# A first block's gates and output matrix, and a first mixer's output matrix, in three passes of rounded parts, with a ring of five slots for the opening's last sixteen

## The chip, the cores and the metric

The kernel runs on one core of one Trainium2 chip, in one launch. The metric is the device time of that core in microseconds (us), the median of three runs.

## The reference, cut to what matters

Two transformer-like blocks over 256 tokens of width 1024, all in float32. The first block runs once; its gates and its output matrix are the last two lines of its mixer:

```python
h = rms_norm(x, norm1_g[l]) * (1.0 + sc1) + sh1
z = h @ w_in[l]
u_val, u_gate, q, k, v, f_logit, gate_c, gate_a = split(z)
conv_out = conv_module(u_val, u_gate, ...)           # 31 taps, layer norm, silu, matrix
attn_out = forgetting_attention(q, k, v, f_logit + b_forget) @ w_attn_out[l]
mixed = sigmoid(gate_c) * conv_out + sigmoid(gate_a) * attn_out
x = x + g1 * (mixed @ w_out[l])
h2 = rms_norm(x, norm2_g) * (1.0 + sc2) + sh2
x = x + g2 * moe_ffn(h2, ...)                        # 32 experts, 4 for each token
```

The second block has two layers. Each is a hybrid mixer (windowed attention and a two-way retention, whose outputs are gated, added and multiplied with `w_out`), then a dense feed-forward part in the first layer and 8 experts in the second.

## The kernel before, in words

The activations stand feature-major: a tile holds 1024 features as 8 pieces of 128 partitions by 256 tokens. Every engine has its own instruction list, written out by hand, and semaphores order them.

**The stream of weight slots.** `plan()` lists the dense matrices in the order of use, cut into slots of 1 MiB (128 x 2048 float32). SP loads them in that order into a ring in the tile `W` (L458): 15 slots for the 50 slots of the first block (the opening), 5 slots from the second block on. A slot is loaded when its predecessor in the ring is free (`free_at`), and since SP works in order, a slot that has to wait holds up all behind it. The opening's stream is 8 slots of `ada0`, then `uqkv_a` (6) and `uqkv_b` (4) with `ada1` and `ada2` (8 each) between them, then `gates` (8), `attn_out` (2), `conv_out` (2) and `w_out` (4): 34 slots and then 16.

**Jobs.** A job multiplies one slot (or half of one) with the activations into one PSUM bank; two banks alternate, and the job after next waits until the bank is read. `feature_job` (L676 to L702) has two forms. A plain one takes float32 operands as they are (L702: 16 products, which the profile shows as 32 matmuls). A split one (L691) takes rounded parts: ACT copies the slot into `WHI_D` in a rounded format (L405), POOL subtracts that from the slot into `WLO_D` (L409, four instructions of 128 x 512), the activations stand likewise in `XHI` and `XLO`, and TensorE makes three passes, high by high, low by high and high by low (48 matmuls). There are four buffers of `WHI_D` and `WLO_D`; the counter `lin_done` counts jobs, `dense_hi` and `dense_lo` count slots split. Before, all split matrices belong to the second block (qa, kva, ret, gg, ffn1, ffn3, ffn2); for them the same memory is laid out as 5 raw slots, 4 high buffers (places 5 to 8 of the ring of 15), 4 low buffers (9 to 12), `XHI` (13) and `XLO` (14).

**The opening.** TensorE runs uqkv, forget, ada(2), and then a hand-written loop over ten steps: a gates job, every second step the attention scores of two heads (L919 to L928), then the values (L948) and the turned probabilities (L937). The scores wait for `negf_ready`, which VectorE (DVE) gives at the end of `log_sigmoid` (L1818 to L1831) and a scan (L2020, L2021). DVE also makes the `ada` products (L1947) and the 31 taps of the convolution, 4 instructions each (L2006): 8 taps just ahead of `log_sigmoid`, and 2 in each step of the loop. ACT reads the banks out (L1549, L1561), and makes the exponentials. Then come attn_out and conv_out, whose products DVE gates (L2069) and adds (L2072), and the four jobs of w_out, with a norm behind them.

**The experts of the first block.** `experts1` (SP, L467): an expert has 12 groups of 1 MiB (8 of `w_exp_in`, 4 of `w_exp_out`), which lie in ring places 3 to 14: groups 0 to 9 in places 5 to 14, groups 10 and 11 in places 3 and 4. The first expert's groups are loaded when the last slot of the stream in that place is free; then SP loads 3 slots of the second block (places 0 to 2), waits for the routing tables, and from there loads group s of the next expert when TensorE has used group s of the expert before (all its chunks). TensorE takes each expert in chunks of 64 tokens: products with the groups at L1102.

**The first mixer** (`mixer2(0)`): after gates and heads, wo_attn (2 slots, 4 jobs) and wo_ret (2 slots, 4 jobs), whose products DVE gates (L2417) and adds (L2439), then w_out0 (4 plain jobs), a first sum behind job 1 (L782), and a norm whose squares go with the later jobs (L1858, L2350, L1861, L2353, L2338, L791). Then ffn1.

```python
def split_dense(eng, q):
    n, _ = split_slots[q]
    if q >= SPLIT_N:
        eng.wait_ge(sem("lin_done"), split_slots[q - SPLIT_N][1])
```

Of the kernel before, what the change touches and what calls it, by code (L numbers as in the profile page):

```python
# [20 lines left out]
F32 = mybir.dt.float32  # L21
# [26 lines left out]
RING = 15  # L48
# [12 lines left out]
class Linear:  # L61


    def __init__(self, name, slots, jobs_per_slot, evac, k_major=0):
# [3 lines left out]
        self.split = name.rstrip("01") in ("qa", "kva", "ret", "gg") or name in ("ffn1", "ffn3", "ffn2")  # L68


def plan():
# [51 lines left out]
    return lins, job_evac, stream, free_at, n_block1, split_slots  # L123
# [17 lines left out]
def build_two_blocks(nc, A, out):  # L141
    lins, job_evac, stream, free_at, N_A, split_slots = plan()
    N_SLOTS = len(stream)
    ctx = ExitStack()
    with ctx:
# [64 lines left out]
        def slot(n):  # L210
            r = n % RING if n < N_A else (n - N_A) % RING2
# [180 lines left out]

        def split_dense(eng, q):
# [54 lines left out]
        def _(sp):  # L448
# [14 lines left out]
            def experts1():  # L463
# [5 lines left out]
                for s in range(12):  # L469
                    wait_free(last_in_ring(ring1(s)))  # L470
# [14 lines left out]
            def experts2():  # L485
# [23 lines left out]
                sp.wait_ge(sem("mix_ready"), 12)  # L509
# [36 lines left out]
        def _(pool):  # L546
# [48 lines left out]
            def mixer2(l):  # L595
                q0 = 52 * l
                for q in range(q0, q0 + 11):
                    if q in (0, 1):
                        pool.wait_ge(sem("m1_split_room"), q + 1)
                    if q == 2:  # L600
                        pool.wait_ge(sem("normed"), 10)
                    split_dense(pool, q)
                for h in range(HEADS):
# [8 lines left out]
                        .then_inc(sem("decay_masked"), 1)  # L612
                    split_dense(pool, q0 + 11 + h)
# [9 lines left out]
                i.then_inc(sem("pool_tables"), 1)  # L623

# [4 lines left out]

            slot_iota(m1)  # L630
            mixer2(0)
            for q in range(19, 52):
# [8 lines left out]
        def _(pe):  # L641
# [38 lines left out]
            def feature_job(lin, s, x, nk=KT, part=0, width=256, ready=None):  # L680

                job = lin.job0 + s * lin.per + part
                if lin.split:
                    q = split_ready(lin, s)
                    bank_free(job)
                    for j in range(width // P):
                        c = part * width + j * P
                        for i, (w, xp) in enumerate(PASSES):
                            w = w[:, q % SPLIT_N, :].rearrange("p (k n) -> p k n", k=KT)
                            for k in range(KT):  # L690
                                mm = pe.matmul(ps(job % 2, T, c0=j * T), w[:, k, c:c + P], xp[:, k, :],  # L691
# [263 lines left out]
            for i in range(10):  # L955
                if i < 8:
                    feature_job(lin, i, H)
# [20 lines left out]
            pe.wait_ge(sem("mix_ready"), 4)  # L978

# [12 lines left out]
            for s in range(4):  # L992
                feature_job(lins["w_out"], s, z(GC, GC + 8))
# [276 lines left out]
            def mixer2(l):  # L1270
# [111 lines left out]
                for s in range(4):  # L1382
                    feature_job(lin, s, z(G2A, G2A + 8), ready=("mix_ready", 4 * l + 5) if s == 0 else None)
# [1140 lines left out]
```

## Time and profile before

| | us |
|---|---|
| median of 3 runs (2340.43 to 2341.96) | 2341.57 |
| the profiled execution's own time | 2340.47 |
| its span in the profile | 2338.7 |
| TensorE busy | 2244.8 (96%) |
| VectorE, ScalarE, GpSimd busy | 714.5, 620.8, 394.1 |
| stage: opening, to the end of w_out | 0 to 262.5 |
| stage: routing and experts of the first block | 262.5 to about 1253 |
| stage: first mixer, to the end of its w_out | about 1280 to 1477 |

The sum of the prediction is made against the profiled execution (2340.47), which is 1.1 us under the median. The clock granted to TensorE is full in nearly the whole span (mean 0.987). The busy shares are averages over stages with different limits, and a busy TensorE can be one with a slow clock, so each stage is read by itself.

### The profile page before, as it was taken

The numbers are of one execution on the slowest core, as the hardware profiler recorded it, in microseconds if no ns is written. First come the engines' busy times: TensorE is split into PE (matmuls) and PEld (weight loads), VectorE is DVE, ScalarE is ACT, GpSimd is POOL, SyncE is SP. The second block draws the span as 40 slices with busy tenths as digits, with TensorE's granted clock in tenths as the row PEclk, the third lists the DMA queues.
The fourth block names the chain that finished last, engine by engine and source line by source line (L and its number), as shares of the span: only waits on it lengthen the run. The fifth ranks groups of instructions, "written<-read, shape, count | busy, mean of one in ns | idle before, by whom it ended". The sixth has DMA issues, their size and how long they took to land.

```text
span 2338.7 us, 36205 instructions
## 1 busy us (share of the span) xinstructions
PE 2244.8 (96%) x13812; PEld 1373.0 (59%) x13813; DVE 714.5 (31%) x1376; ACT 620.8 (27%) x903; POOL 394.1 (17%) x371
## 2 busy tenths in 40 slices
PE   7999999999999999999998999999999999999898
PEld 5887744444444444444446988899998863333333
DVE  4864322222222222222225244312315341111013
ACT  2143111111111111112124671443458011111111
POOL 2000000000000000000003761688586000000000
PEclk9999999999999999999999999999999999999999
DMA  9973399999999999989994533555454475999652
GB/s 359 381 259 110 101 411 418 418 418 418 418 418 418 417 418 418 418 363 380 418 418 167 179 109 108 180 183 180 127 180 117 155 287 216 402 405 396 276 230 84
DMA packets 223487, 688.71 MB, mean 294 GB/s; under 512 B 28330, under 2 KB 117362, under 8 KB 187570
## 3 DMA queue, kind: packets, MB, share of 16 engines
q1 hardware_dynamic: 221776, 685.82, 76.4%
q10 hardware_dynamic: 1490, 1.61, 0.2%
q8 instruction: 56, 0.92, 0.2%
q0 software_dynamic: 144, 0.20, 0.0%
q14 instruction: 21, 0.17, 0.0%
HBM read 686.53 MB, written 1.05 MB: 294 GB/s over the span
## 4 chain that ended last, share of the span: by engine, by line
PE 72%; DMA 11%; SPq 11%; DVE 3%; issue 2%; ACT 1%; POOL 0%; ACTq 0%; DVEq 0%; POOLq 0%
PE PS L1102 17%; PE PS L702 12%; DMA RAW<-in_w_exp_in 10%; PE PS L691 6%; SPq L467 6%; PE PS L1206 6%; PE PS L676 6%; PE PS L1066 4%; PE PS L1217 3%; SPq L489 3%; PE PS L1407 3%; PE PS L1085 2%; PE PS L748 1%; PE PS L1113 1%; SPq L497 1%
## 5 line engine op out<-in xcount | busy, mean ns | idle before, releaser
L1102 PE MATMUL PS<-RAW,Z 128*64 128x512 f32 x3168 | 713.3, 597 | 24.1 <-DMA RAW<-in_w_exp_in 23.2
L409 POOL TENSOR_TENSOR WLO_D<-W,WHI_D 128x512 fp32r<-128x512 f32 x284 | 360.2, 1304 | 1159.6 <-ACT SPARE L1632 965.9
L1102 PEld LDWEIGHTS PS<-RAW,Z 128*64 128x64 f32 x3168 | 213.7, 136 | 454.7 <-issue 376.8
L1206 PE MATMUL PS<-W,Z 128*64 128x512 f32 (+1 forms) x1056 | 212.5, 558 | 10.9 <-DMA W<-in_moe_w 10.2
L702 PE MATMUL PS<-Z,W 128*128 128x256 f32 x768 | 170.1, 382 | 1.5 <-DVE Z L2072 1.5
L405 ACT ACTIVATE WHI_D<-W 128x2048 fp32r<-128x2048 f32 x71 | 135.3, 1908 | 114.0 <-DMA W<-in_ffn_w 42.3
L1206 PEld LDWEIGHTS PS<-W,Z 128*64 128x64 f32 x1056 | 74.5, 137 | 148.9 <-issue 129.6
L702 PEld LDWEIGHTS PS<-Z,W 128*128 128x128 f32 x768 | 146.4, 191 | 23.0 <-DVE Z L2072 1.9
L1066 PE MATMUL PS<-Z 128*128 128x64 f32 x1088 | 125.3, 273 | 0.0
L1066 PEld LDWEIGHTS PS<-Z 128*128 128x128 f32 x1088 | 124.2, 192 | 0.2 <-issue 0.2
L2194 DVE TENSOR_TENSOR Z<-Z,PS 128x1024 f32<-128x1024 f32 x66 | 80.4, 1218 | 126.0 <-PE PS L1085 126.0
L702 PE MATMUL PS<-H,W 128*128 128x256 f32 x512 | 118.2, 393 | 0.0
L1642 ACT ACTIVATE Z<-PS 128x512 f32<-128x512 f32 x33 | 19.7, 597 | 360.5 <-PE PS L1102 360.5
L1217 PE MATMUL PS<-W,Z 128*64 128x512 f32 x484 | 111.1, 599 | 0.0
L702 PEld LDWEIGHTS PS<-H,W 128*128 128x128 f32 x512 | 100.7, 198 | 14.5 <-issue 0.2
L2220 DVE COPY Z<-PS 128x512 f32<-128x512 f32 x33 | 22.8, 692 | 280.2 <-PE PS L1102 280.2
L2297 DVE TENSOR_TENSOR Z<-PS,Z 128x512 f32<-128x512 f32 (+1 forms) x22 | 10.5, 520 | 249.3 <-ACT Z L1678 249.3
L1650 ACT ACTIVATE SQ<-PS 128x512 f32<-128x512 f32 x33 | 19.7, 597 | 252.2 <-PE PS L1102 252.2
L2183 DVE TENSOR_SCALAR Z<-Z,SQ 128x128 f32 x66 | 19.9, 344 | 208.3 <-PE PS L1075 208.3
L1085 PEld LDWEIGHTS PS<-Z,SQ 64*128 64x128 f32 x536 | 46.1, 186 | 57.4 <-issue 54.5
L1085 PE MATMUL PS<-Z,SQ 64*128 64x256 f32 x536 | 76.0, 402 | 0.7 <-ACT Z L1619 0.7
L1217 PEld LDWEIGHTS PS<-W,Z 128*64 128x64 f32 x484 | 31.8, 136 | 57.6 <-issue 57.6
(405 smaller groups left out, 2692.8 us busy)
## 6 DMA issues: line engine op xcount, KB each, us to landing
RAW<-in_w_exp_in SPq DMA_DIRECT2D x256, 1024.0 KB, 19.2
RAW<-in_w_exp_out SPq DMA_DIRECT2D x128, 1024.0 KB, 21.7
W<-in_moe_w SPq DMA_DIRECT2D x128, 704.0 KB, 15.7
W<-in_w_in SPq DMA_DIRECT2D x52, 1024.0 KB, 5.4
W<-in_moe_w SPq DMA_DIRECT2D x40, 1024.0 KB, 15.9
W<-in_ffn_w SPq DMA_DIRECT2D x33, 1024.0 KB, 5.3
W<-in_w_ada SPq DMA_DIRECT2D x24, 1024.0 KB, 14.2
W<-in_w_out SPq DMA_DIRECT2D x12, 1024.0 KB, 5.0
```

Of the source, the lines that this page charges most:

```text
L405: eng.activation(hi, raw, ACT.Copy).then_inc(sem("dense_hi"), 1)
L409: i = eng.tensor_tensor(lo[:, c:c + 512], raw[:, c:c + 512], hi[:, c:c + 512].bitcast(F32), ALU.subtract)
L467: sp.dma_start(dst, src).then_inc(sem(f"raw{s}"), 16)
L676: mm = pe.matmul(ps(gate_bank(l, i), T, c0=j * T), w[:, k, j * P:(j + 1) * P], xp[:, k, :], start=(n == k == 0), stop=(n == 2 and k == KT ...
L691: mm = pe.matmul(ps(job % 2, T, c0=j * T), w[:, k, c:c + P], xp[:, k, :], start=(i == k == 0), stop=(i == 2 and k == KT - 1))
L702: mm = pe.matmul(ps(job % 2, T, c0=j * T), w[:, k, c:c + P], x[:, k, :], start=(k == 0), stop=(k == nk - 1))
L1066: mm = pe.matmul(ps(2, HALF, c0=k * HALF), HT[:, a, k * P:(k + 1) * P], PICK[:, a, 0:HALF], start=(a == 0), stop=(a == 1))
L1085: mm = pe.matmul(ps(6 + h, T, c0=j * T), YS1[64 * h:64 * h + 64, c:c + P], GT[64 * h:64 * h + 64, :], start=True, stop=True)
L1102: mm = pe.matmul(ps(bank, 512, 64 * h, 64 * h + 64), x, w[:, c:c + 512], start=first, stop=final, skip_group_check=True)
L1206: mm = pe.matmul(o if b < 2 else o.rearrange("p (i n) -> p i n", i=2), X1[:, s, :], rhs, start=(s == 0), stop=(s == 7), skip_group_check=True)
L1217: mm = pe.matmul(ps(3, 512, 64 * h, 64 * h + 64), x, second2(j)[:, c:c + 512], start=(i == j == 0), stop=(j == 5), skip_group_check=True)
L2194: dve.tensor_tensor(o, o, PS[:, 6:8, :].rearrange("p h (k t) -> p h k t", k=2), ALU.add)\
```

## The change

It adds gates, w_out and w_out0 to the split matrices (16 slots more, each with a round on ACT and a subtraction on POOL), and makes `XHI` and `XLO` from H for the gates and from the mixed sums for the two output matrices. To have room for the parts, the opening's last 16 slots (from gates on) go through the first five places of the ring; places 5 to 14 are the parts. The first expert's groups 0 to 3 now wait for jobs 1 to 4 of w_out, and the groups behind them for job 4.

```diff
-        self.split = name.rstrip("01") in ("qa", "kva", "ret", "gg") or name in ("ffn1", "ffn3", "ffn2")
+        self.split = name.rstrip("01") in ("qa", "kva", "ret", "gg") or name in ("ffn1", "ffn3", "ffn2", "gates", "w_out", "w_out0")
+    n_opening = 8 + 6 + 8 + 4 + 8
-            r = n % RING if n < N_A else (n - N_A) % RING2
+            r = n % RING if n < N_O else (n - N_O) % RING2 if n < N_A else (n - N_A) % RING2
 def split_dense(eng, q):
             if q >= SPLIT_N:
                 eng.wait_ge(sem("lin_done"), split_slots[q - SPLIT_N][1])
+            else:
+                name, count = free_at[last_use(RING2 + q + (0 if eng is nc.scalar else SPLIT_N))]
+                eng.wait_ge(sem(name), count)
 SP, experts1:
                 for s in range(12):
-                    wait_free(last_in_ring(ring1(s)))
+                    r = ring1(s)
+                    if r < RING2:
+                        wait_free(last_in_ring(r))
+                    else:
+                        sp.wait_ge(sem("lin_done"), lins["w_out"].group0 + ((r - RING2) % SPLIT_N + 1 if r < 13 else 4))
                     group(s, 0)
 SP, stream:
-                if n >= RING:
-                    wait_free(n - RING)
+                older = [k for k in range(n) if slot(k)[1] == slot(n)[1]]
+                if older:
+                    wait_free(older[-1])
 POOL, ahead of the experts:
+            split_dense(pool, 0)
+            pool.wait_ge(sem("in_hi"), 1)
+            for p in range(4):
+                o = slice(2 * p, 2 * p + 2)
+                i = pool.tensor_tensor(XLO[:, o, :], H[:, o, :], XHI[:, o, :].bitcast(F32), ALU.subtract)
+            i.then_inc(sem("in_lo"), 1)
+            for q in range(1, 12):
+                split_dense(pool, q)
             slot_iota(m1)
             mixer2(0)
-            for q in range(19, 52):
+            for q in range(QF["w_out0"], QF["qa1"]):
                 split_dense(pool, q)
 PE:
-                    feature_job(lin, i, H)
+                    feature_job(lin, i, H, ready=(("in_hi", 1, 0), ("in_lo", 1, 0)) if i == 0 else None)
-            pe.wait_ge(sem("mix_ready"), 4)
-                feature_job(lins["w_out"], s, z(GC, GC + 8))
+                feature_job(lins["w_out"], s, None, ready=(("in_hi", 2, 1), ("in_lo", 2, 1)) if s == 0 else None)
+                    if l == 0:
+                        feature_job(lin, s, None, ready=(("in_hi", 6, 1), ("in_lo", 6, 1)) if s == 0 else None)
 ACT, opening (s == 8 is the evacuation of the ninth uqkv job):
+                if s == 8:
+                    name, count = free_at[last_use(13)]
+                    act.wait_ge(sem(name), count)
+                    act.activation(XHI[:, :, :], H[:, :, :], ACT.Copy).then_inc(sem("in_hi"), 1)
+                    split_dense(act, 0)
+            split_dense(act, 1)
             b = linear_ready(lins["forget"], 0)
 ...
             act.activation(SQ[0:8, 2 * T:3 * T], SQ[0:8, T:2 * T], ACT.Exp, scale=-1.0).then_inc(sem("logsig_exp"), 1)
+            for q in (2, 3):
+                split_dense(act, q)
 ...
+                if i < 5:
+                    split_dense(act, 4 + i)
 ...
+            def mix_high(p, g0, n):
+                act.wait_ge(sem("mix_sum"), n)
+                act.activation(XHI[:, 2 * p:2 * p + 2, :], z(g0 + 2 * p, g0 + 2 * p + 2), ACT.Copy).then_inc(sem("in_hi"), 1)
+            for q in (9, 10):
+                split_dense(act, q)
+            for p in range(4):
+                mix_high(p, GC, p + 1)
+                if p == 1:
+                    split_dense(act, 11)
 ACT, mixer2:
                 root(SQ[:, 0:T])
                 if l == 0:
-                    for q in range(19, 19 + SPLIT_N):
+                    for q in range(QF["w_out0"], QF["w_out0"] + SPLIT_N):
+                        split_dense(act, q)
+                    for p in range(4):
+                        mix_high(p, G2A, p + 5)
+                    for q in range(QF["ffn1"], QF["ffn1"] + 3):
                         split_dense(act, q)
                 norm_root()
             final_x(2, V_LN1G, V_LN1B)
+            split_dense(act, QF["ffn1"] + 3)
 DVE (the same in mixer2(0), with G2A and 4 + j; every l = 1 wait on mix_ready is now on in_lo):
+            def mix_low(p, g0, n):
+                dve.wait_ge(sem("in_hi"), n + 1)
+                dve.tensor_tensor(pair(XLO, p), z(g0 + 2 * p, g0 + 2 * p + 2), pair(XHI, p).bitcast(F32), ALU.subtract)\
+                    .then_inc(sem("in_lo"), 1)
-                            dve.tensor_tensor(o, o, z(GA + t, GA + t + 2), ALU.add).then_inc(sem("mix_ready"), 1)
+                            dve.tensor_tensor(o, o, z(GA + t, GA + t + 2), ALU.add).then_inc(sem("mix_sum"), 1)
+                            if t:
+                                mix_low(t // 2 - 1, GC, t // 2)
+                if g0 == GC:
+                    mix_low(3, GC, 4)
```

## Rows read from the trace of the kernel before

**Rows 1.** The page: GB/s in 40 slices, and the costliest group of instructions.
```profile
GB/s 359 381 259 110 101 411 418 418 418 418 418 418 418 417 418 418 418 363 380 418 418 167 179 109 108 180 183 180 127 180 117 155 287 216 402 405 396 276 230 84
...
L1102 PE MATMUL PS<-RAW,Z 128*64 128x512 f32 x3168 | 713.3, 597 | 24.1 <-DMA RAW<-in_w_exp_in 23.2
```

**Rows 2.** Timeline of SP: start us, duration us, queue, line, transfer, count.
```profile
262.96 12.01 SPq L458 DMA_DIRECT2D W<-in_w_in  x9
289.30 12.85 SPq L467 DMA_DIRECT2D RAW<-in_w_exp_in  x8
...
317.39 12.85 SPq L467 DMA_DIRECT2D RAW<-in_w_exp_in  x8
```

**Rows 3.** Windows: busy us by engine, granted clock, DMA share, GB/s.
```profile
118.00:120.00 2.00, 2.00 (x6) 1.64 (x7) 1.77 (x2) 1.45 (x2) 0.00 (x0) 0.50 1.10 347
...
290.00:295.00 5.00, 5.00 (x26) 1.57 (x24) 1.10 (x5) 0.38 (x1) 0.00 (x0) 1.00 0.89 323
295.00:300.00 5.00, 5.00 (x26) 1.71 (x24) 0.00 (x0) 0.00 (x0) 0.00 (x0) 1.00 1.01 362
300.00:305.00 5.00, 5.00 (x38) 3.40 (x35) 2.38 (x4) 2.42 (x3) 0.00 (x0) 1.00 1.00 424
```

**Rows 4.** The chain of waits: start us, duration us, what.
```profile
118.19 9.26 PE PS L702 x32
...
131.09 6.91 PE PS L702 x32
```

**Rows 5.** Timeline of DVE ahead of the first scores.
```profile
104.32 12.75 DVE L2006 SCALAR_TENSOR_TENSOR Z<-W,VEC,Z 128x256 f32<-128x256 f32 x32
...
120.29 0.41 DVE L1824 TENSOR_TENSOR SQ<-SQ 8x256 f32<-8x256 f32 x1
...
126.92 0.28 DVE L2021 TENSOR_SCALAR W<-SQ 8x256 f32<-8x256 f32 x1
```

**Rows 6.** Timeline of ACT over the readings of the last two uqkv jobs.
```profile
103.02 0.60 ACT L1549 ACTIVATE Z<-PS 128x512 f32<-128x512 f32 x1 [6.31 <-PE PS L756]
109.92 0.60 ACT L1549 ACTIVATE Z<-PS 128x512 f32<-128x512 f32 x1 [6.31 <-PE PS L756]
```

**Rows 7.** Two single lines by duration, ns: min/median/max.
```profile
L405 ACT ACTIVATE WHI_D<-W x71: 1895/1908/1918, 1225.2 to 1802.7; 128x2048 fp32r<-128x2048 f32 x71
...
L2353 DVE SCALAR_TENSOR_TENSOR X<-X,SQ x9: 684/692/1801, 1460.9 to 1879.0; 128x512 f32<-128x512 f32 x9
```

**Rows 8.** DMA issues: transfer, count, KB each, median us to landing.
```profile
W<-in_w_in SPq DMA_DIRECT2D x52, 1024.0 KB, 5.4
```

**Rows 9.** Timeline of POOL: two splits.
```profile
1334.62 4.96 POOL L409 TENSOR_TENSOR WLO_D<-W,WHI_D 128x512 fp32r<-128x512 f32 x4 [2.87 <-PE PS L676]
...
1457.44 6.30 POOL L409 TENSOR_TENSOR WLO_D<-W,WHI_D 128x512 fp32r<-128x512 f32 x4 [1.93 <-ACT WHI_D L405]
```

**Rows 10.** Timeline of DVE beside these two splits.
```profile
1338.40 1.21 DVE L2380 TENSOR_SCALAR ST<-ST 128x2 f32<-128x2 f32 x1
...
1460.85 5.27 DVE L2353 SCALAR_TENSOR_TENSOR X<-X,SQ 128x512 f32<-128x512 f32 x3
```

**Rows 11.** Timeline of PE in ffn1: first passes of two split jobs.
```profile
1500.61 1.12 PE L691 MATMUL PS<-XHI,WHI_D 128*128 128x256 f32 x8
...
1506.37 1.12 PE L691 MATMUL PS<-XHI,WHI_D 128*128 128x256 f32 x8
```

**Rows 12.** Timeline of PE at w_out of the first block.
```profile
233.51 14.08 PE L702 MATMUL PS<-Z,W 128*128 128x256 f32 x64 [1.51 <-DVE Z L2072]
...
262.45 0.43 PE L791 MATMUL PS<-SQ,ONES 128*32 128x64 f32 x16
```

**Rows 13.** Timeline of SP and DVE at the first mixer's end.
```profile
1391.86 44.70 SPq L458 DMA_DIRECT2D W<-in_w_out  x4
...
1450.01 0.69 DVE L2336 SCALAR_TENSOR_TENSOR X<-X,PS 128x512 f32<-128x512 f32 x1 [5.49 <-PE PS L702]
...
1477.05 0.69 DVE L2338 TENSOR_TENSOR X<-X,PS 128x512 f32<-128x512 f32 x1 [7.56 <-PE PS L702]
```

More of the change, by code:

```diff
@@ L122, in plan @@
             free_at.append(("lin_done", lin.group0 + (s + 1) * (1 if lin.k_major else lin.per)))
-    return lins, job_evac, stream, free_at, n_block1, split_slots
+    q_first = {}
+    for q, (n, _) in enumerate(split_slots):
+        q_first.setdefault(stream[n][0], q)
+    return lins, job_evac, stream, free_at, n_opening, n_block1, split_slots, q_first
 class Chain:
@@ L141, in build_two_blocks @@
 def build_two_blocks(nc, A, out):
-    lins, job_evac, stream, free_at, N_A, split_slots = plan()
+    lins, job_evac, stream, free_at, N_O, N_A, split_slots, QF = plan()
     N_SLOTS = len(stream)
@@ L391, in msem, with last_use @@
             return sem(f"{m.tag}_{name}")
+        def last_use(r):
+            return max(n for n in range(N_O) if slot(n)[1] == r)
         def split_dense(eng, q):
@@ L508, in experts2 @@
                     second(j, 0)
-                sp.wait_ge(sem("mix_ready"), 12)
+                sp.wait_ge(sem("in_lo"), 13)
                 first(7, 0)
@@ L595, in mixer2 @@
             def mixer2(l):
-                q0 = 52 * l
+                q0 = QF[f"qa{l}"]
                 for q in range(q0, q0 + 11):
-                    if q in (0, 1):
-                        pool.wait_ge(sem("m1_split_room"), q + 1)
-                    if q == 2:
+                    if l == 0 and q - q0 in (0, 1):
+                        pool.wait_ge(sem("m1_split_room"), q - q0 + 1)
+                    if l == 0 and q - q0 == 2:
                         pool.wait_ge(sem("normed"), 10)
@@ L690, in feature_job @@
                             for k in range(KT):
+                                if ready and j == 0 and i != 1 and k % 2 == 0:
+                                    pe.wait_ge(sem(ready[i // 2][0]), ready[i // 2][1] + k // 2 * ready[i // 2][2])
                                 mm = pe.matmul(ps(job % 2, T, c0=j * T), w[:, k, c:c + P], xp[:, k, :],
@@ L1654, in experts1 @@
                     chunk(g)
-                chunk(last, lambda: [split_dense(act, q) for q in range(2)])
+                chunk(last, lambda: [split_dense(act, QF["qa0"] + q) for q in range(2)])
                 turned(count)
@@ L1780, in _ @@
                 act.activation(z(2 * s, 2 * s + 2), ps2(b), ACT.Silu).then_inc(sem("evac_act"), 1)
-                split_dense(act, 19 + SPLIT_N + s)
+                split_dense(act, QF["ffn1"] + SPLIT_N + s)
             for s in range(11):
-                split_dense(act, 30 + SPLIT_N + s)
+                split_dense(act, QF["ffn3"] + SPLIT_N + s)
                 act.wait_ge(sem("evac_dve"), job_evac[lins["ffn3"].job0 + s][1])
                 act.activation(FHI[:, 2 * s:2 * s + 2, :], hidden_raw(s), ACT.Copy).then_inc(sem("ffn_hi"), 1)
-            for q in range(41 + SPLIT_N, 54):
+            for q in range(QF["ffn2"] + SPLIT_N, QF["qa1"] + 2):
                 split_dense(act, q)
@@ L1790, in _ @@
             final_x(3, V_LN2G, V_LN2B)
-            for q in range(54, 56):
+            for q in range(QF["qa1"] + 2, QF["qa1"] + SPLIT_N):
                 split_dense(act, q)
@@ L2438, in mixer2 @@
                     o = z(G2A + 2 * j, G2A + 2 * j + 2)
-                    dve.tensor_tensor(o, o, z(G2R + 2 * j, G2R + 2 * j + 2), ALU.add).then_inc(sem("mix_ready"), 1)
+                    dve.tensor_tensor(o, o, z(G2R + 2 * j, G2R + 2 * j + 2), ALU.add).then_inc(sem("in_lo" if l else "mix_sum"), 1)
+                    if l == 0 and j:
+                        mix_low(j - 1, G2A, 4 + j)
+                if l == 0:
+                    mix_low(3, G2A, 8)
                 residual_norm(lins[f"w_out{l}"])
```

14 lines of the change are left out of this document (10 added, 4 removed).

## The prediction

> **What bounds the kernel now.** I read the page first, then each stage where the diff touches it. [rows 1]: from the seventh slice of the span (292 us) to the seventeenth the DMA engines move 418 GB/s, a ceiling, and the expert matmuls L1102 idled 24.1 us in all, 23.2 of them ended by a DMA. An expert is 12 MiB, 12.58 MB, so 30.1 us at 418 GB/s, or 2.51 us for 1 MiB; the first experts on TensorE, where nothing is late, run at 317.39 - 289.30 = 28.1 us, the pace at which SP's issues follow it [rows 2]. So in the middle of the expert stage the loads set the pace, 2 us an expert behind TensorE. The last such stretch ends with the eighteenth slice (363 GB/s). From there TensorE needs its own time to the stage's end. The end therefore hangs on when the stream of loads starts. It starts late: w_out ends at 262.5, SP issues nine transfers then [rows 2], the ring is full by about 280, and the next loads wait for the experts: 323 GB/s in 290 to 295, 362, then 424 [rows 3]. These ten us moved what 8.2 us at 418 do ((323 + 362) x 5 / 418), so the stream is one that starts at 291.9 and runs at 418, 29.4 us behind w_out.
>
> Ahead of this, TensorE bounds the opening: the chain goes through gates job 0 (9.26 us, at half the clock, 0.50, up to about 122), then scores, then job 1 (6.91) [rows 3, 4]. DVE is just in time beside it: eight taps from 104.32, then log-sigmoid and scan, whose last instruction ends at 127.20 [rows 5], 0.3 us ahead of job 0's end. In the mixer TensorE waits little. So three things count: what comes between 104 and 127, each job's length, and the gap from w_out to the stream of loads.
>
> **The change, part by part.** The forecast is a sum over six terms.
>
> *1. Work beside the taps: +21.7.* ACT reads the ninth uqkv job at 103.02 [rows 6], then rounds H and slot 0, each 128 x 2048, 1.91 us, and POOL starts at about 107.4. It has split 0, the low part of H and split 1, 12 instructions of 128 x 512; the second slot waits for the last uqkv job (about 109.8) and lands 5.4 us later, with its high part at about 117 [rows 7, 8], in time for POOL, which takes 12 x 1.24 = 14.9 us. A split costs POOL 4.96 when nothing disturbs it and 6.30 beside DVE's L2353 [rows 9]. And beside POOL's split DVE suffers: three L2353 took 5.27, 1.76 each, where the median of this line is 0.69; a 128 x 2 instruction took 1.21 us [rows 7, 10]. I read this as DVE waiting out one whole POOL instruction before each of its own that reads two operands from SBUF (or runs as a tensor_scalar): 1.76 - 0.69 = 1.07. (The Trainium skill, "SBUF — State Buffer", "Who interferes with whom", says that GpSimd and VectorE share a port pair under a lock held for a whole instruction, and that a VectorE instruction with at most one SBUF input doesn't contend; the trace agrees with the first, 1.07 being nearly one 1.24 us instruction.) The taps read W and Z, both in SBUF. Between two POOL instructions one tap gets in, so the period is 1.24 + 0.27 = 1.51 for one tap where 0.41 was [rows 5]: +1.10 for each of 12 POOL instructions, +13.2; the taps end at 130.3. Log-sigmoid starts behind them; after its exponential ACT rounds slots 2 and 3, and POOL's 8 instructions stand beside L1824 to L1830, 8 x 1.05 = +8.4. The scan's end moves from 127.2 to 148.9, +21.7, and with it the first scores and all behind them on TensorE, for job 0 was over long before. Bounds: with no lock ACT's own copies ahead of the forget logits cost +0.9; with a full 1.24 for each of 20 instructions, +25.
>
> *2. A cold clock: +1.8.* TensorE then idles for some 20 us behind job 0. It came out of its wait before ada(2) at 0.50 too, and job 0 took 9.26 where others take 6.91 [rows 3, 4]: 2.35 lost. Here the scores and the next job are what runs slow, a little less of it: 1.8, bounds 0 and 2.4.
>
> *3. Gates jobs 1 to 7: -8.0.* A split job is 1506.37 - 1500.61 = 5.76 us [rows 11], a plain one 6.91: -1.15 for each of seven; job 0's saving lies in the wait of term 1. Splits must keep up: 1.91 on ACT and 4.96 on POOL for a step of over 10 us. The slots come in time (5 in the ring, 5.4 to land). If POOL's four instructions fall into the taps of the loop, eight in a step, DVE loses up to 4.4 for a pair of steps, of which I think its slack takes all; the bound is in a rival.
>
> *4. w_out: -3.7.* Four jobs in 28.2 (two took 14.08) [rows 12] become four of 5.76, -1.15 each, -4.6. Against this, the first product now waits for the ACT copy of the last sum and DVE's subtraction behind it: about +0.9, from 0.60 for an ACT instruction of 128 x 512 [rows 6] and a share of a wait for POOL. Bounds -4.6 and -2.
>
> w_out's end: 21.7 + 1.8 - 8.0 - 3.7 = +11.8, at 274.3.
>
> *5. The preload of the experts: +8.0 more.* Before, at w_out's end only the last places were still to be loaded. Now places 8 to 14 hold the parts until w_out's job 4, so nine groups and three slots, 12 MiB, are issued at its end. From there: 0.4 to the first issue, 1.9 until data flow (my estimate: a slot lands 5.4 after its issue [rows 8], less 2.51 is 2.9 at most), 9 x 2.51 = 22.6 for the groups, and 12.5 for the last expert's small pieces and the slots behind, as the 12.01 us of issue at 262.96 shows [rows 2]: 37.4 behind w_out against 29.4. TensorE isn't kept waiting much, but the stream starts 8.0 later against it, and through the DMA-bound stretch that is carried to the end. Bounds: 5 (the small pieces overlap) and 12 (they run at half the rate). (The same page's "SBUF: two separate sides" gives about 358 GB/s between HBM and a core; the trace shows 418 over ten slices [rows 1]. By the page, 1 MiB would be 2.93 us and this term +11.8; I keep the trace's.)
>
> Experts' end: +19.8.
>
> *6. First mixer: +2.6.* Of w_out0's four slots, issued from 1391.86, the last waits for wo_ret's first slot and goes at 1436.56 [rows 13]; it lands 5.0 later and ACT rounds it by about 1444. The copies of the sums stand behind all four rounds on ACT, and DVE blocks in its first subtraction behind them, so wo_ret's last two products are gated late. Job 0, which ended at 1449.96, just ahead of DVE's reading at 1450.01 [rows 13], ends at about 1455.5, +5.6; three split jobs give back 3.5, and the norm's DVE chain beside POOL's splits keeps about 0.5: +2.6 at job 3's end (1477.0 before). Bounds: -4.6, when nothing is late, and +5. ffn1's start is not moved by it: a slot costs POOL 5.0 and a job 5.76.
>
> The sum: 11.8 + 8.0 + 2.6 = +22.4 against the profiled execution's 2340.47: 2362.9. The median of the runs stands 1.1 above it: 2364.
>
> **The rivals.**
>
> *No lock on the taps (A).* The rows with the lock are of other shapes and lines; no row shows the taps beside POOL. Then term 1 is +0.9, term 2 is nothing, job 0 gains its 1.15 only in part: w_out's end -11.8, loads +8.0, and the mixer, whose norm then loses nothing either, +0.6: -3.2, 2338.4, which is not slower. For it: nothing but the missing row. Against it: a 128 x 2 instruction paying 1.21. Decides: whether the taps at 107 to 122 take above 0.45 each. 0.11.
>
> *The lock, but a late preload costs nothing (B).* If the loads that are still missing at w_out's end are hidden behind routing and the first experts, term 5 is 0: +14.4, 2356. Against it: 323 and 362 GB/s in [rows 3] show the stream already held by TensorE, with no slack stored. 0.10.
>
> *Both gone (C).* -11.2, 2330.4. 0.04.
>
> *The loop becomes VectorE's (D).* If splits 4 to 8 fall beside the taps and softmax sums and nothing absorbs it, up to 4.4 for each of two or more steps: +9 to the sum, 2373. For it: DVE was 0.3 from being late once. 0.12.
>
> That the change doesn't do what it says I leave at 0.01: L691 and its operands run 71 slots in this kernel already.
>
> **How the numbers follow.** The forecast, terms 1 to 6, has 0.62; its own range, from the bounds of terms 5 and 6 mostly, is 2354 to 2371. The range reaches down to take in B and a part of the case between it and A (a lock of half the size is 2353), and up to D: 2347 to 2373; outside are A, C, D's upper half. A measurement of this kernel can tell 0.2%, 4.7 us, from no change. Faster: C and the lower third of A, 0.07. Same: the rest of A, 0.08. Slower: 0.85.
>
> **What would show it.** Right: L2006's first 32 taps at over 20 us in place of 12.75; the first scores (L919) at about 149; granted clock under 1 right behind; gates jobs of 5.8 in L691 in place of L702; w_out's end at 274; the GB/s of 274 to 310 high without a break, and the experts' idle for DMA above 23.2; w_out0's first job late for the high part of the sums. The forecast falls if the taps keep 0.41 beside POOL (A), if the experts' end moves by no more than w_out's (B), or if TensorE waits in the gates loop for the scores' probabilities (D).

## The result and the profile after

The changed kernel takes 2362.79 us (median of 4 runs, 2362.09 to 2364.78) where the kernel before takes 2341.00 in the same runs: 1.0097 of it, 95% interval 1.0084 to 1.0109, slower by 21.8 us. 2364 was forecast, and the range was 2347 to 2373. The sum came out right, but not all its terms did, as the stages show. The profiled execution took 2362.09, 21.6 above the one read before. In the table both executions are cut at the same events in TensorE's rows:

| stage, on TensorE | before, us | after, us | difference | forecast |
|---|---|---|---|---|
| start to the first scores | 127.37 | 145.55 | +18.2 | +21.7 |
| to attn_out | 76.53 | 69.61 | -6.9 | -6.2 |
| to w_out's last job | 58.55 | 55.06 | -3.5 | -3.7 |
| to the experts' end | 989.70 | 997.65 | +8.0 | +8.0 |
| to the first qa job | 16.93 | 13.32 | -3.6 | none |
| to the last job of w_out0 | 207.86 | 216.75 | +8.9 | +2.6 |
| rest | | | +0.6 | none |

The first stage, read on VectorE (start us, us, line and operation, count, and in brackets the idle time ahead and what ended it):

```profile
103.77 12.75 DVE L2065 SCALAR_TENSOR_TENSOR Z<-W,VEC,Z 128x256 f32<-128x256 f32 x32
122.77 1.28 DVE L1877 SCALAR_TENSOR_TENSOR SQ<-SQ 8x256 f32<-8x256 f32 x1 [6.25 <-ACT SQ L1591]
...
132.07 9.77 DVE L1887 SCALAR_TENSOR_TENSOR SQ<-SQ 8x256 f32<-8x256 f32 x7
...
145.12 0.28 DVE L2080 TENSOR_SCALAR W<-SQ 8x256 f32<-8x256 f32 x1
```

The 32 taps take 12.75 us, to the hundredth what they took before [rows 5]. Log-sigmoid starts 6.25 us after VectorE is free, and its row of seven instructions takes 9.77 us. In the kernel before the same row was:

```profile
121.50 3.09 DVE L1828 SCALAR_TENSOR_TENSOR SQ<-SQ 8x256 f32<-8x256 f32 x7
```

GpSimd, beside it (the first row from a narrow window, so that it stands alone):

```profile
111.12 6.53 POOL L420 TENSOR_TENSOR WLO_D<-W,WHI_D 128x512 fp32r<-128x512 f32 x1 [69.35 <-ACT WHI_D L416]
...
121.28 5.21 POOL L655 TENSOR_TENSOR XLO<-H,XHI 128x512 fp32r<-128x512 f32 x4
126.45 16.51 POOL L420 TENSOR_TENSOR WLO_D<-W,WHI_D 128x512 fp32r<-128x512 f32 x12
```

Its first subtraction takes 6.53 us and ends at 117.65, 1.1 us after the last tap: here GpSimd waited for VectorE. The other 19 (three of slot 0, four of the input, twelve of slots 1 to 3) follow without a gap to 142.96. Slot 0's four are over at 121.3, before log-sigmoid starts; the last 15 run beside it. ACT, at the forget logits:

```profile
120.47 1.91 ACT L416 ACTIVATE WHI_D<-W 128x2048 fp32r<-128x2048 f32 x1 [6.20 <-DMA W<-in_w_in]
122.29 0.45 ACT L1591 ACTIVATE SQ<-PS,BFG 8x256 f32<-8x256 f32 x1
```

The reading of the forget logits (L1591) stands behind the round of slot 1, which had landed only at 120.5. The clock of TensorE behind its wait of 14.9 us (in windows: the busy time of the five engines, then the granted clock, the DMA share and GB/s):

```profile
145.00:150.00 5.00, 4.45 (x18) 3.36 (x19) 0.45 (x3) 0.00 (x0) 0.00 (x0) 0.53 0.50 190
150.00:155.00 5.00, 5.00 (x42) 4.92 (x41) 4.35 (x13) 3.54 (x6) 0.70 (x1) 1.00 0.02 5
```

The scores run at half the clock (0.53 in the first window) and the next job at the full one (1.00). The scores take 5.33 us (145.55 to 150.88) where they took 3.56 (127.37 to 130.93): 1.8 more, the size of term 2, though term 2 put a part of it on the next job. The experts, on the page:

```profile
GB/s 361 306 163 72 235 378 417 418 418 418 418 418 418 418 418 418 418 412 344 418 418 191 179 108 143 108 197 180 143 161 126 136 290 233 385 404 392 285 224 87
...
L1131 PE MATMUL PS<-RAW,Z 128*64 128x512 f32 x3168 | 716.2, 597 | 30.6 <-DMA RAW<-in_w_exp_in 29.7
```

The same ceiling of 418 for as long [rows 1], and 29.7 us of idle time for loads in place of 23.2. SP:

```profile
251.96 20.97 SPq L478 DMA_DIRECT2D RAW<-in_w_exp_in  x8
272.97 4.72 SPq L478 DMA_DIRECT2D RAW<-in_w_exp_out  x4
277.73 26.04 SPq L469 DMA_DIRECT2D W<-in_w_in  x9
```

Nine of the expert's groups and the nine transfers of the second block go out behind w_out's last job (270.2), where before only the nine transfers were left [rows 2]. And the mixer's end, in TensorE's timeline at w_out0's first job:

```profile
1459.48 0.71 PE L722 MATMUL PS<-XHI,WHI_D 128*128 128x256 f32 x4 [2.96 <-DVE Z L2486]
1461.18 0.80 PE L722 MATMUL PS<-XHI,WHI_D 128*128 128x256 f32 x2 [0.98 <-ACT XHI L1632]
1464.53 0.79 PE L722 MATMUL PS<-XHI,WHI_D 128*128 128x256 f32 x2 [2.55 <-ACT XHI L1632]
1465.12 1.91 PE L722 MATMUL PS<-XHI,WLO_D 128*128 128x256 f32 x8
```

Three waits, 6.5 us together, and then passes of 1.91 us where 1.12 is usual [rows 11]: the granted clock stood at 0.50 from 1464 to 1469. Job 0 ends at 1472.4, not at 1455.5 + 12 = 1467.5, which would be the forecast shifted by the late start of the mixer (12.1 us).

### The profile page after: what moved, and what is told of

Read it like the earlier page. It is cut to its first block, busy times and chain, and to the rows that moved or that the text cites. A ratio compares the mean times of both kernels' runs of the same rounds, so it can differ in the third digit from the quotient of the medians.

```text
span 2360.3 us, 36855 instructions
## 1 busy us (share of the span) xinstructions
PE 2233.7 (95%) x14068; PEld 1369.7 (58%) x14069; DVE 754.5 (32%) x1384; ACT 656.8 (28%) x928; POOL 492.1 (21%) x439
## 4 chain that ended last, share of the span: by engine, by line
PE 65%; DMA 14%; SPq 11%; DVE 6%; issue 2%; ACT 1%; POOL 0%; ACTq 0%; DVEq 0%; POOLq 0%
PE PS L1131 13%; DMA RAW<-in_w_exp_in 12%; PE PS L722 9%; SPq L478 8%; PE PS L1235 7%; PE PS L733 7%; PE PS L705 6%; PE PS L1246 4%; PE PS L1095 3%; PE PS L1439 3%; PE PS L1114 2%; PE PS L779 1%; SPq L504 1%; PE PS L1142 1%; PE PS L1193 1%
## 5 line engine op out<-in xcount | busy, mean ns | idle before, releaser
L1131 PE MATMUL PS<-RAW,Z 128*64 128x512 f32 x3168 | 716.2, 597 | 30.6 <-DMA RAW<-in_w_exp_in 29.7
L420 POOL TENSOR_TENSOR WLO_D<-W,WHI_D 128x512 fp32r<-128x512 f32 x348 | 453.0, 1341 | 1282.6 <-ACT SPARE L1686 973.9
L1235 PEld LDWEIGHTS PS<-W,Z 128*64 128x64 f32 x1056 | 74.4, 137 | 150.0 <-issue 129.7
L733 PE MATMUL PS<-Z,W 128*128 128x256 f32 x512 | 112.6, 380 | 1.2 <-DVE Z L2500 1.2
L722 PE MATMUL PS<-XHI,WHI_D 128*128 128x256 f32 x656 | 98.3, 293 | 14.4 <-ACT XHI L1632 5.5
L1246 PE MATMUL PS<-W,Z 128*64 128x512 f32 x484 | 111.1, 599 | 0.0
L733 PEld LDWEIGHTS PS<-Z,W 128*128 128x128 f32 x512 | 97.0, 190 | 15.3 <-DVE Z L2500 1.6
L722 PEld LDWEIGHTS PS<-XHI,WHI_D 128*128 128x128 f32 x656 | 87.9, 198 | 16.5 <-ACT XHI L1632 6.4
L722 PE MATMUL PS<-XHI,WLO_D 128*128 128x256 f32 x656 | 95.1, 289 | 0.0
L722 PE MATMUL PS<-XLO,WHI_D 128*128 128x256 f32 x656 | 93.8, 286 | 0.8 <-DVE XLO L2124 0.5
L722 PEld LDWEIGHTS PS<-XHI,WLO_D 128*128 128x128 f32 x656 | 87.9, 199 | 0.0
L722 PEld LDWEIGHTS PS<-XLO,WHI_D 128*128 128x128 f32 x656 | 86.2, 195 | 1.2 <-DVE XLO L2124 0.7
```

What stands on the lines that cost most here:

```text
L420: i = eng.tensor_tensor(lo[:, c:c + 512], raw[:, c:c + 512], hi[:, c:c + 512].bitcast(F32), ALU.subtract)
L1131: mm = pe.matmul(ps(bank, 512, 64 * h, 64 * h + 64), x, w[:, c:c + 512], start=first, stop=final, skip_group_check=True)
L1235: mm = pe.matmul(o if b < 2 else o.rearrange("p (i n) -> p i n", i=2), X1[:, s, :], rhs, start=(s == 0), stop=(s == 7), skip_group_check=True)
L1246: mm = pe.matmul(ps(3, 512, 64 * h, 64 * h + 64), x, second2(j)[:, c:c + 512], start=(i == j == 0), stop=(j == 5), skip_group_check=True)
```

## The experiments

All comparisons are with the kernel before, run on the same chip; it took 2342.05 beside the first four, 2340.86 beside the next four, 2339.96 and 2340.66 beside the last two pairs. The 95% intervals reach about 2 us to each side for the kernels with 11 or 12 runs, and 4 us for those with four (e1, e3, e4). Where less matters, the stages of the profiled execution are read; that is one execution of each kernel, and two executions of the same stage can differ, as is said where it counts.

**e1_sums_first.** In the first mixer ACT makes the high parts of the sums ahead of the round of the fourth slot.

```diff
-                    for q in range(QF["w_out0"], QF["w_out0"] + SPLIT_N):
+                    for q in range(QF["w_out0"], QF["w_out0"] + 3):
                         split_dense(act, q)
                     for p in range(4):
                         mix_high(p, G2A, p + 5)
+                    split_dense(act, QF["w_out0"] + 3)
```

> The changed kernel with one edit in the first mixer: on ACT the four high parts of the sums stand ahead of the round of w_out0's fourth slot, not behind it. Theory: the order on ACT costs the mixer most of its +9.1 us (job 0 of w_out0 ended at 1472.4, its first passes waiting for the copies of the sums, and TensorE came out of these waits at half the clock). The copies then follow the sums by 0.6 us, w_out0's job 0 ends near 1462, and the run comes out 8 to 10 us below the changed kernel's 2362.8, near 2354. Rival: the late landing of the slots, or VectorE waiting for GpSimd's subtractions, sets job 0's end; then the run stays within 2 us of 2362.8. If the fourth slot's round becomes what job 3 waits for, only half comes back.

2356.24 us (2352.66 to 2357.96; 1.0060, interval 1.0043 to 1.0077), 6.6 below the changed kernel, where 8 to 10 had been expected.

```profile
1457.51 1.06 PE L722 MATMUL PS<-XHI,WHI_D 128*128 128x256 f32 x6
1460.03 0.50 PE L722 MATMUL PS<-XHI,WHI_D 128*128 128x256 f32 x2 [1.46 <-ACT XHI L1632]
```

One wait of 1.46 is left of 6.5, and the passes behind it run at full clock. From the first product of wo_ret (L1401 here, L1372 in the kernel before) to job 3's end it is 52.0 us, against 61.5 in the changed kernel and 52.5 before. So the mixer's cost was the order on ACT and the cold clock that its waits brought. Its size varies with the execution: e3, e4 and e5, which keep the order, take 59.2, 61.4 and 59.1. In e3 the waits are 2.99, 0.98 and 2.55 us, the same, but the passes are back at 1.11 us from 1468.2 on and not from 1471.4. So the 9.5 between these two profiles is more than the medians show.

**e2_before_late_loads.** The kernel before, with the waits of the changed one ahead of the first expert's groups.

```diff
                 for s in range(12):
-                    wait_free(last_in_ring(ring1(s)))
+                    r = ring1(s)
+                    if r < 5:
+                        wait_free(last_in_ring(r))
+                    else:
+                        sp.wait_ge(sem("lin_done"), lins["w_out"].group0 + ((r - 5) % 4 + 1 if r < 13 else 4))
```

> The kernel before with one edit: the first expert's groups in ring places 5 to 14 wait for w_out's jobs 1 to 4 as in the changed kernel, everything else as it was. Theory (term 5): the stream of loads starts 8 us later against TensorE and the DMA-bound stretch carries that to the end, so 2341 + 8 = 2349, with w_out's end still at 262.5 and the experts' end at about 1260. Rival B: the late loads are hidden behind routing and the first experts, 2341 to 2343, and the 8 us between w_out's end and the experts' end of the changed kernel came from something else.

2349.41 us (2346.34 to 2351.38; 1.0030, interval 1.0020 to 1.0041). Job 3 of w_out ends, and the experts end, at:

```profile
264.35 0.43 PE L795 MATMUL PS<-SQ,ONES 128*32 128x64 f32 x16
...
1262.04 1.55 PE L824 MATMUL PS<-ONES 128*128 128x512 f32 x3
```

That is 997.7 us where the kernel before has 989.7 and the changed one 997.65. The late loads cost 8.0 us in this stage and 7.4 in the medians, so nothing of them is hidden: rival B is out.

**e3_forget_first.** The changed kernel; ACT rounds slot 1 together with slots 2 and 3, behind the exponential.

```diff
-            split_dense(act, 1)
             b = linear_ready(lins["forget"], 0)
...
-            for q in (2, 3):
+            for q in (1, 2, 3):
                 split_dense(act, q)
```

> The changed kernel with one edit: ACT rounds slot 1 behind the exponential of log-sigmoid, so the reading of the forget logits no longer stands behind the landing of slot 1. Theory: of the +18.2 us at the first scores, 5.7 are this wait (VectorE idle from 116.5 to 122.8) and 12.4 are log-sigmoid's own instructions beside GpSimd's subtractions, which stay: the first scores come 5 to 6 us earlier than 145.5 and the run at about 2357. Rival: what sets the first scores is the end of GpSimd's 16 subtractions (143.0), whenever log-sigmoid starts; then nothing is gained, 2362 to 2363.

2358.97 us (2357.22 to 2361.14; 1.0070, interval 1.0053 to 1.0087), 3.8 below the changed kernel. The first scores come at 143.61, only 1.9 earlier, and w_out's end only 0.5 earlier; 2.3 us of the rest are the mixer's clock, as said under e1. VectorE, then GpSimd:

```profile
117.23 1.48 DVE L1875 SCALAR_TENSOR_TENSOR SQ<-SQ 8x256 f32<-8x256 f32 x1
...
126.65 9.88 DVE L1885 SCALAR_TENSOR_TENSOR SQ<-SQ 8x256 f32<-8x256 f32 x7
```

```profile
107.11 15.26 POOL L420 TENSOR_TENSOR WLO_D<-W,WHI_D 128x512 fp32r<-128x512 f32 x4 [66.58 <-ACT WHI_D L416]
...
127.70 16.89 POOL L420 TENSOR_TENSOR WLO_D<-W,WHI_D 128x512 fp32r<-128x512 f32 x12
```

Log-sigmoid starts 5.5 us earlier and every instruction of it up to the last one (143.4) now stands beside a subtraction. The chain takes 26.2 us (117.23 to 143.43) in place of 22.6, and eats most of what the early start gave: the wait for slot 1 cost 1.9 and not 5.7. The rival is nearly right in its number but not in its reason: the scores came 1.0 us before the last subtraction ended (144.6), so it is VectorE's slowed chain that sets them. e1, whose opening is that of the changed kernel, says the same without an edit: its last uqkv job was over earlier, slot 1 landed at 116.5, log-sigmoid started at 118.84 and not at 122.77, and the first scores still came at 145.11.

**e4_pool_holds.** e3_forget_first, and GpSimd waits for the scan's end before slot 1.

```diff
             i.then_inc(sem("in_lo"), 1)
+            pool.wait_ge(sem("negf_ready"), 1)
             for q in range(1, 12):
```

> The kernel of e3_forget_first with one more edit: GpSimd waits for the end of the scan (negf_ready) before it subtracts slot 1, so that beside log-sigmoid stand only the subtractions of slot 0 and of the input, 8 in place of 16. Theory of the lock: log-sigmoid's instructions fall back to 0.28 to 0.45 us once GpSimd is through with the input's low part (near 126.5), the scan ends near 132 to 133, the first scores some 6 to 7 us ahead of e3_forget_first; job 1 then waits up to 1 us for slot 1's low part: about 2351. Rival, no lock but slowness of small SBUF instructions beside ACT's rounds or DMA: log-sigmoid keeps 1.3 us for each and the run stays within 1 us of e3_forget_first or is slower for the wait of job 1.

2358.83 us (2356.09 to 2359.58; 1.0065, interval 1.0048 to 1.0081), no better than e3_forget_first, where 2351 had been expected. The first half came, and larger than expected: the first scores are 10.0 us earlier (133.61 against 143.61). Then 8.6 of them were lost again before attn_out:

```profile
126.80 4.05 DVE L1886 SCALAR_TENSOR_TENSOR SQ<-SQ 8x256 f32<-8x256 f32 x7
...
138.41 11.52 DVE L2064 SCALAR_TENSOR_TENSOR Z<-W,VEC,Z 128x256 f32<-128x256 f32 x8
```

```profile
152.49 0.90 PE L969 MATMUL PS<-IDENT,SQ 128*128 128x128 f32 x3 [7.95 <-DVE SQ L2088]
```

With a subtraction beside its first instruction alone (GpSimd is through with the input at 127.9), log-sigmoid's row takes 4.05 in place of 9.88. GpSimd's subtractions are all that was moved, so the slowness is theirs, and not that of small instructions beside ACT's rounds or the loads. The subtractions now stand beside the first taps of the loop: eight taps take 11.52 us, 1.44 each, where all eight usually take 3.25, and TensorE waits 7.95 us for the probabilities behind them. This is rival D, at the price that the prediction gave for two steps (8.8), in a kernel with the work shifted.

**e5_gates_plain.** The changed kernel with plain gates: neither H nor a gates slot is in parts, the ring of five stays.

```diff
-        self.split = name.rstrip("01") in ("qa", "kva", "ret", "gg") or name in ("ffn1", "ffn3", "ffn2", "gates", "w_out", "w_out0")
+        self.split = name.rstrip("01") in ("qa", "kva", "ret", "gg") or name in ("ffn1", "ffn3", "ffn2", "w_out", "w_out0")
...
```

The rest of the edit takes out the rounds and subtractions of the gates and sets the counters that follow.

> The changed kernel with the gates as plain jobs again (in the ring of five, w_out and w_out0 still in parts). Theory: log-sigmoid has no subtraction beside it, the first scores come at 127 to 129 and not at 145.5; the gates loop takes its 76.5 us again and not 69.6; w_out still saves 3.5; so w_out ends near 260 (270.2 in the changed kernel), the late loads (+8) and the mixer (+9) stay: about 2352. The split of the gates is then worth +11 by itself. Rival: the ring of five, not the subtractions, holds up the opening (slots of the gates land late), and w_out still ends at 265 or later, 2357 or more.

2348.53 us (2346.97 to 2352.12; 1.0037, interval 1.0025 to 1.0049), 14.3 below the changed kernel, where 11 had been expected. TensorE at the first scores, w_out's end and the experts' end:

```profile
127.63 0.49 PE L942 MATMUL PS<-Z 64*128 64x128 f32 x4 [4.58 <-DVE W L2065]
...
259.17 0.43 PE L814 MATMUL PS<-SQ,ONES 128*32 128x64 f32 x16
...
1256.37 1.98 PE L843 MATMUL PS<-ONES 128*128 128x512 f32 x4
```

The first scores are back where they were, w_out ends 11.1 us earlier than in the changed kernel, and 997.2 us lie between the last two rows. The split of the gates costs 11 us by itself, and the ring of five holds up nothing. Of the other 3 us, 2.4 are in the mixer (59.1 against 61.5, as said under e1).

**e6_mixer_alone.** The kernel before with w_out0 alone in parts, in e1's order; opening and expert loads are as they were. (The edit is to the tuple of split matrices, to the ring, which has 15 places for all 50 slots again, and to the counters that follow.)

> The kernel before with w_out0 alone in parts, the copies of the sums ahead of the fourth slot's round (as in e1_sums_first), opening and expert loads as they were. Theory: the mixer's end takes 52.0 us where it took 52.5 from wo_ret to job 3, so nothing that can be measured: 2340 to 2342. Rival: without the late stream and the slow opening the split's full -4.6 comes through, 2337; or the mixer is slower by what e1 left, over 2343.

2340.72 us (1.0001, interval 0.9992 to 1.0010): no change. The mixer from wo_ret to job 3 takes 52.0 us again. Each of three later jobs saves 1.15, and a wait of 3.55 (2.63 before) for VectorE's squares of job 1 stands behind job 2, with a cold clock behind it.

**e7_before_moment_late, e8_mixer_moment_late.** TensorE takes the sums of job 1's squares behind job 3, in the kernel before and in e6.

```diff
                         moments(X, H, 0, True, False, 5, 4)
-                        moments(X, H, 1, False, False, 5, 4)
+                moments(X, H, 1, False, False, 5, 4)
                 moments(X, H, 2, False, False, 5, 4)
```

> The kernel before with one edit in the mixers: TensorE's sums of job 1's squares (they wait 2.6 us for VectorE, whose L2353 stands beside GpSimd's split, and TensorE comes out at half the clock) stand behind job 3, not ahead of it. Theory: wait and slow clock of the first mixer go, -3.7, the second has no such wait (no subtraction beside it): 2337.5. Rival: VectorE's chain only ends the norm as late as before, 2341.

> e6_mixer_alone with the edit of e7_before_moment_late. Theory: in the split form the same wait was 3.5 us with some 3 at half the clock behind it, so -6 against e6_mixer_alone, 2335, the one version here below the kernel before, and 2 to 3 below e7 for w_out0's three passes. Rival: VectorE's norm chain beside GpSimd's splits becomes the end (its squares of job 3 late): no better than e7.

2338.93 us (0.9990, interval 0.9981 to 0.9999) and 2338.98 (0.9992, 0.9983 to 1.0001). In e7 TensorE still waited, one step later, for job 1's bank, and then for the last squares:

```profile
1466.63 7.14 PE L702 MATMUL PS<-Z,W 128*128 128x256 f32 x32 [1.75 <-DVE X L2338]
...
1476.24 0.43 PE L791 MATMUL PS<-H,ONES 128*32 128x64 f32 x16 [1.22 <-DVE H L1861]
```

From wo_ret to ffn1 it is 56.5 us, against 57.8 before. But single executions can't carry that difference: e2, e9 and e11, whose mixer is that of before, take 58.0, 58.0 and 56.3. In e8, where the wait for the bank is 2.66, that stretch takes 54.4, and 55.7 and 55.0 in e10 and e12 with the same mixer (57.3 in e6). So the three passes and the later sums together do bring something in the stage, 2 to 3 us, of which the medians show 2. My 2335 was wrong: VectorE's chain beside the subtractions keeps the rest.

**e9_nops, e10_late_nops, e11_more_matmuls, e12_late_more_matmuls.** These are on a stage that had no term in the forecast, the 3.6 us between experts and qa. In the kernel before (the rows are of e9) TensorE stands still behind the experts for 3.24 us, and the profile names nothing that it waits for ("issue"); in the changed kernel it does not:

```profile
1260.42 0.40 PE L793 MATMUL PS<-Z,ONES 128*32 128x64 f32 x14
1264.06 0.80 PE L793 MATMUL PS<-Z,ONES 128*32 128x64 f32 x18 [3.24 <-issue]
```

```profile
1276.71 0.63 PE L822 MATMUL PS<-Z,ONES 128*32 128x64 f32 x32
```

> The kernel before with 128 empty instructions at the head of TensorE's list, where it waits 9.9 us for its first data; nothing else. In every kernel whose TensorE list is as long as before up to the norm behind the experts (before, e2, e6, e7, e8) TensorE stands still for 3.23 us with nothing to wait for, at the same instruction, and comes out at half the clock; in every kernel with gates or w_out in parts (after, e1, e3, e4, e5) it doesn't. Theory: it is the load of a piece of TensorE's instructions, whose place depends on how many instructions stand ahead, and the changed kernel gained its 3.7 us there by chance; the empty instructions move it too: from the experts' end to the first qa job 13.3 us and not 16.9, and 2341 - 3.7 = 2337. Rival: it has to do with the parts (GpSimd, rounds, other data at that time), and the stall stays where it is: 2341. Third: the stall goes there and comes up at another place: 2341 too, with a shorter stretch here.

> e8_mixer_moment_late with the same 128 empty instructions. Theory: the stall of 3.2 us and the slow clock behind it go, 2339 - 3.7 = 2335, below both kernels by more than the measurement's error. Rival: as for e9_nops, 2339.

The empty instructions left no mark (36205 instructions in the profile of e9 and of the kernel before), so e9_nops is taken as the kernel before once more (2340.75 against 2339.96 for itself, a measure of how well two equal kernels agree) and e10_late_nops is e8 once more (2338.07; 0.9990, 0.9981 to 0.9999). They tell nothing of the stall. The second pair, e11 on the kernel before and e12 on e8, has real products instead:

```diff
             pe.wait_ge(sem("ident_ready"), 1)
+            for _i in range(128):
+                pe.matmul(ps(1, 4, 0, 32), ONES[:, 0:32], ONES[:, 0:4], start=True, stop=True)
```

> The kernel before with 128 tiny products (32 columns by 4) at the head of TensorE's list, as many as w_out in parts adds ahead of the experts; e9's empty instructions left no mark in the trace, so that run said nothing. Theory: the stall of 3.2 us behind the experts lies where a piece of TensorE's instructions ends, and moves when instructions are added ahead of it, as in the changed kernel: 13.3 us and not 16.9 from the experts' end to the first qa job; the head may cost up to 4 us where the tiny products run on past the first data, so the total lies between 2336 and 2341 and says less than that stretch. Rival: the stall has to do with gates or w_out in parts (other engines or data), and stays: 16.9.

> e8_mixer_moment_late with the same 128 tiny products. Theory: the stall goes here too, so it lies below e8's 2339 by 3.7 less what the head costs: 2335 to 2339, below both kernels. Rival as for e11_more_matmuls: 2339 and the stall where it was.

2339.67 us (1.0000, 0.9991 to 1.0008) and 2338.94 (0.9994, 0.9984 to 1.0005). The stall stayed in both, one product later than in all the others (behind 15 of the 32 and not behind 14), in e11:

```profile
1262.05 0.40 PE L791 MATMUL PS<-Z,ONES 128*32 128x64 f32 x15
1265.68 0.47 PE L791 MATMUL PS<-Z,ONES 128*32 128x64 f32 x17 [3.24 <-issue]
```

So the added products neither took the stall away nor moved it out of these 32 products. That doesn't rule out every form of the theory. In the profile the 128 float32 products stand as 256 matmuls (14068 against 13812), while w_out in parts adds 64: the two kernels weren't equally long up to the stall, as had been meant. And the DMA view shows a packet of each of the two instruction queues, q8 and q14, inside the gap in the kernel before, e2 and e11, while in the changed kernel and in e5 such packets come one at a time and TensorE doesn't stand still. That fits a load of instructions, but doesn't show it as the cause. All seven kernels with a plain w_out in the opening have the stall (before, e2, e6, e7, e8, e11, e12, and the repeats e9 and e10). All five with w_out in parts lack it (after, e1, e3, e4, e5). Late loads (e2) and plain gates (e5) make no difference. What links the two stays open.

## Why the prediction came out right, and where its steps were wrong

*Term 1 (+21.7, though its parts 13.2 and 8.4 make 21.6; measured +18.2).* The mechanism, VectorE and GpSimd shutting each other out, is right, and it is the largest cost of the change: e5 takes it away, e4 moves it. The step that failed is the taps, +13.2 of the 21.7: "Between two POOL instructions one tap gets in" did not hold there. The taps were already running back to back when the first subtraction came, and GpSimd got in only when they were over (6.53 us for one instruction), so they cost nothing. Rival A had this half right, at 0.40 us a tap, but it gave log-sigmoid no lock either. Log-sigmoid didn't keep its pace: 19 of the 20 subtractions were pushed behind the taps, 15 of them and not 8 stood beside log-sigmoid, and its rows took 22.6 us in place of 10.2 (+12.4 against my +8.4). The rest, a start 5.8 us later than before behind slot 1, I had as "in time", since I let the slot go at 109.8 and not with this execution's last uqkv job at 113.6; e3 shows that only 1.9 of it counted, for an earlier start makes the chain longer. That 13.2 us too many and 9.8 too few left an error of only 3.5 is luck.

The Trainium skill, "SBUF — State Buffer", "Who interferes with whom", says that the issue order and not the shape of an operation decides who blocks. The traces agree: the same taps went undisturbed at 104 to 117 and took 1.44 us each in e4, where the subtractions were there first. What I had not expected is that VectorE's stream without gaps keeps GpSimd out for all the rest of its length: 5.4 us here, and some 10 in e3, where the first subtraction started at 107.11 and took 11.31 us. It isn't so the other way round. GpSimd's stream in e4 let one tap in at each step. Why a waiting subtraction gets in behind each tap there, and not in the changed kernel, no run here shows.

*Terms 2 and 3 (-6.2; -6.9).* Right. The scores ran at half the clock, for the 1.8 us of term 2. Jobs 1 to 7 cost 5.76 each. VectorE's slack took the subtractions of the loop: beside them the probabilities' line took 12.8 us in sum where it took 4.4, and TensorE waited 0.3 for it. e4 shows that there was little to spare.

*Term 4 (-3.7; -3.5), term 5 (+8.0; +8.0).* Right, and e2 shows term 5 by itself to 0.1 us. The figure of the Trainium skill, "SBUF — State Buffer", "SBUF: two separate sides", about 358 GB/s, would have given 11.8 for term 5; the slices stand at 418 after as before.

*Term 6 (+2.6; +8.9).* Mechanism right, size wrong: the copies behind the four rounds, VectorE blocked by its first subtraction, wo_ret's last products gated late. The fourth slot was rounded at 1456.8, within 1 us of the forecast shifted by 12. From there job 0 took 15.6 us to its end and not 11.5: the last two sums came one after the other with 2.55 us of wait between their copies, and TensorE came out of its waits at half the clock (the 42 products from 1464.53 took 7.8 us, where 42 x 0.12 is 5.0), which I had priced for the opening (term 2) and forgot here. The waits had begun earlier, too: wo_ret itself stood 1.17 us for VectorE's sum beside the first two subtractions, which the kernel before doesn't have. Behind it the three jobs gave back 1.4 and not 3.5, since the wait for the squares of job 1 grew from 2.63 to 3.52 and the slow passes behind it lost 2.1 us where they had lost 1.1 (4.96 us up to 1494.97 for three passes of 0.96; before, 8.14 for a job of 7.07). Both bounds (-4.6 and +5) missed it. In e3 and e5 the same stretch came 2.3 to 2.4 us shorter, so some 6.5 to 9 is what the order costs.

*What was in no term.* The stall of 3.2 us behind the experts went, -3.6 us with the clock; why it went stays open. So the forecast's 22.4 against 21.6 is terms 1 and 6 off by -3.5 and +6.3, and a gain that nobody could read from the trace of before, -3.6. The ways in which the parts cost time were mostly right; that the sum agrees to 1 us is luck. A sum says less than its stages.

No version here beats the kernel before by more than the 0.2% that a measurement can tell. e8, its repeat e10 and e12 stand at 2338 to 2339, 1.7 to 1.9 us (under 0.1%) below it in each comparison, and e7 is 1.9 below it too, without any part of the change.

## What to carry to other kernels

Count what a helper engine's new work stands beside, and ask who is there first. Here VectorE's stream without gaps shut GpSimd out; GpSimd's stream let VectorE in once per instruction, and a chain of small dependent VectorE instructions lost about one whole GpSimd instruction at every step. Moving such work only pays where there is slack on both sides; e4 moved it out of one critical stretch into the next and got nothing. Where a stream of loads is the bound for hundreds of microseconds, price every early use of its buffers by how much later it starts; and where a wait is added ahead of TensorE, add the cold clock behind it.

## What had not been expected of the hardware

VectorE's 32 taps of 0.40 us kept a GpSimd subtraction waiting from 111.1 to 116.5, and the same line took 1.44 a tap where the subtractions came first. Small instructions (8 partitions by 256) lose as much as large ones: 1.24 to 1.40 us each for 0.28 to 0.44. And TensorE was at the forget logits anywhere from 107 to 114 us in the executions of these kernels. Its clock falls at different moments of the first 100 us: in the changed kernel's execution (forget logits at 113.57) the granted clock was 0.50 from 30 to 40 us and 0.66 from 80 to 90, in e5's (107.07) 1.00 and 0.97. That may be a part of the 5 to 7 us by which single runs of one kernel differ. The first scores wait for VectorE and so hide some of it (127.1 to 130.3 in the kernels with the opening as before).
